# Prompt attention: the causal mask added in PSUM by VectorE instead of by a third product on TensorE

## The reference, cut to what matters

```python
def block(i):
    start = i * Q_BLOCK                                   # Q_BLOCK = 128
    logits = (jnp.einsum('bqhd,bkhd->bhqk', qb, k) * scale
              + (fq[..., None] - f_cum[:, :, None, :]))
    qpos = start + jnp.arange(Q_BLOCK)
    logits = jnp.where(qpos[:, None] >= key_pos[None, :], logits, -jnp.inf)
    probs = jax.nn.softmax(logits, axis=-1).astype(v.dtype)
    return jnp.einsum('bhqk,bkhd->bqhd', probs, v)
```

## Time and profile before

| | before |
|---|---|
| median of 3 runs | 3169.92 us (3169.56 to 3171.61) |
| the profiled execution, own time | 3169.61 us |
| its span in the trace | 3168.0 us |
| TensorE busy in the span | 3096.5 us, 98% |
| VectorE, ScalarE, GpSimd busy | 1558.5, 910.9, 261.2 us |

### The profile page before, as it was taken

The page is one execution under the profiler, slowest core; times in us unless marked ns, Lnnn a source line. Parts: engine busy times, 40 slices in busy tenths (PEclk is TensorE's granted clock), DMA queues, the critical chain, the costliest instruction groups (busy, mean ns, idle before and its releaser), DMA issues.

```text
span 3168.0 us, 52161 instructions
## 1 busy us (share of the span) xinstructions
PE 3096.5 (98%) x20550; PEld 2968.3 (94%) x20550; DVE 1558.5 (49%) x2693; ACT 910.9 (29%) x1670; POOL 261.2 (8%) x317
## 2 busy tenths in 40 slices
PE   8999999999999999999999998999999999999999
PEld 8999999999999999999987776559999999999998
DVE  4444284444444447543335555552844444544472
ACT  4111351111111116422225554343511111111262
POOL 1000010000000001000015542210100000000011
PEclk9999999999999999999999999999999999999999
DMA  2111111111111111113227774971111111111112
GB/s 99 47 47 41 47 37 45 47 47 41 47 47 41 47 61 39 42 47 118 70 46 162 131 135 172 386 300 51 41 47 41 47 47 41 47 47 40 61 48 70
DMA packets 234057, 238.93 MB, mean 75 GB/s; under 512 B 18806, under 2 KB 191862, under 8 KB 233859
## 3 DMA queue, kind: packets, MB, share of 16 engines
q1 hardware_dynamic: 209842, 156.26, 16.9%
q0 software_dynamic: 24016, 79.77, 8.5%
HBM read 201.11 MB, written 18.10 MB: 69 GB/s over the span
## 4 chain that ended last, share of the span: by engine, by line
PE 80%; DVE 4%; issue 2%; ACT 2%; DMA 1%; POOL 0%; DVEq 0%; SPq 0%; ACTq 0%; POOLq 0%
PE psum L2082 21%; PE psum L2084 21%; PE psum L2083 21%; PE psum L2638 3%; PE psum L2108 2%; PE psum L2102 2%; PE psum L2103 2%; PE psum L2622 2%; PE psum L2607 1%; PE psum L2608 1%; PE psum L2688 1%; PE psum L2740 1%; DVE xs_lo L1563 1%; PE psum L2717 0%; PE psum L2649 0%
## 5 line engine op out<-in xcount | busy, mean ns | idle before, releaser
L2082 PE MATMUL psum<-xs_hi,w_hi 128*128 128x384 f32 (+1 forms) x2784 | 911.6, 327 | 2.7 <-DVE w_lo L1339 2.4
L2084 PE MATMUL psum<-xs_hi,w_lo 128*128 128x384 f32 (+1 forms) x2784 | 908.0, 326 | 0.0
L2083 PE MATMUL psum<-xs_lo,w_hi 128*128 128x384 f32 (+1 forms) x2784 | 907.3, 326 | 0.0
L2082 PEld LDWEIGHTS psum<-xs_hi,w_hi 128*128 128x128 f32 x2784 | 522.7, 188 | 3.9 <-DVE w_lo L1339 3.7
L2083 PEld LDWEIGHTS psum<-xs_lo,w_hi 128*128 128x128 f32 x2784 | 522.7, 188 | 0.0
L2084 PEld LDWEIGHTS psum<-xs_hi,w_lo 128*128 128x128 f32 x2784 | 522.5, 188 | 0.0
L782 ACT ACTIVATE w_hi<-raw 128x1024 fp32r<-128x1024 f32 x192 | 202.4, 1054 | 622.3 <-DVEq L1355 598.4
L2084 PE MATMUL psum<-hid_hi,w_lo 128*128 128x384 f32 (+1 forms) x1056 | 346.0, 328 | 0.0
L2082 PE MATMUL psum<-hid_hi,w_hi 128*128 128x384 f32 (+1 forms) x1056 | 345.6, 327 | 0.0
L2083 PE MATMUL psum<-hid_lo,w_hi 128*128 128x384 f32 (+1 forms) x1056 | 345.1, 327 | 0.0
L1696 DVE TENSOR_TENSOR y<-y,psum 128x384 f32<-128x384 f32 x528 | 268.6, 530 | 155.3 <-PE psum L2084 155.3
(11 more groups left out here) (311 smaller groups left out, 4104.9 us busy)
## 6 DMA issues: line engine op xcount, KB each, us to landing
kpage<-in_cache_k SPq DMA_DIRECT2D x64, 512.0 KB, 8.5
v_page<-in_cache_v POOLq DMA_DIRECT2D x64, 512.0 KB, 5.7
raw<-in_w_gate SPq DMA_DIRECT2D x44, 512.0 KB, 3.7
raw<-in_w_up SPq DMA_DIRECT2D x44, 512.0 KB, 3.7
raw<-in_w_down SPq DMA_DIRECT2D x44, 512.0 KB, 3.8
raw<-in_w_in SPq DMA_DIRECT2D x24, 512.0 KB, 3.6
raw<-in_w_ple_gate SPq DMA_DIRECT2D x16, 512.0 KB, 3.8
k_hh<-kT_scratch POOLq DMA_DIRECT2D x32, 256.0 KB, 6.5
```

The costliest lines, as they stand in the source:

```text
L2082: M(out, wh, xh, start=first, stop=False)
L2083: M(out, wh, xl, start=False, stop=False)
L2084: return M(out, wl, xh, start=False, stop=last)
```

## The change

The third product is gone; the second product of the last part ends the sum and raises `s_ready`. VectorE adds the mask `causal` to the last 128 columns in PSUM, in place, raises `s_masked`, waits for it and takes the maximum. Ahead of the stage VectorE waits for `consts` to reach 6. The copies `causal_r` and `ident_r` and TensorE's wait for them go.

```diff
--- before.py
+++ after.py
@@ -168,8 +168,6 @@
     convT = misc("convT", [P, C, 2 + 2 * NB])
 
     causal = sb("causal", [P, P], F32, off)
-    causal_r = sb("causal_r", [P, P], F32R, off + 512)
-    ident_r = sb("ident_r", [P, P], F32R, off + 1024)
     wf_raw = misc("wf_raw", [P, C, H])
     wf_hi = misc("wf_hi", [P, C, H], F32R)
     wf_lo = misc("wf_lo", [P, C, H], F32R)
@@ -302,7 +300,7 @@
         fs_stored = sem("fs_stored")
         v_stored = sem("v_stored")
 
-        aug_one, mask_ready = sem("aug_one"), sem("mask_ready")
+        aug_one, s_masked = sem("aug_one"), sem("s_masked")
         head_landed = [sem(f"head_landed{i}") for i in range(2)]
         head_raw_landed = sem("head_raw_landed")
         aug_landed = [sem(f"aug_landed{i}") for i in range(2)]
@@ -1207,9 +1205,6 @@
             for hh in range(2):
                 A(k_low[hh][DH:DH + 4, :], k_raw[DH:DH + 4, :], ACT.Copy).then_inc(aug_one, 1)
                 A(q_high[hh][DH:DH + 4, :], k_raw[DH:DH + 4, :], ACT.Copy, scale=-1.0).then_inc(aug_one, 1)
-            act_e.wait_ge(consts, 6)
-            A(causal_r[:, :], causal[:, :], ACT.Copy).then_inc(mask_ready, 1)
-            A(ident_r[:, :], ident[:, :], ACT.Copy).then_inc(mask_ready, 1)
             for tb in range(NTB):
                 if tb == 8:
                     act_e.wait_ge(fs_stored, 32)
@@ -1919,8 +1914,13 @@
                 row(TR_V, tb)
 
 
+            dve.wait_ge(consts, 6)
+
             def maxes(i):
                 dve.wait_ge(s_ready, i + 1)
+                diag = slice(QBS[i % NI] * P, (QBS[i % NI] + 1) * P)
+                V.tensor_tensor(s_view(i)[:, diag], s_view(i)[:, diag], causal[:, :], ALU.add).then_inc(s_masked, 1)
+                dve.wait_ge(s_masked, i + 1)
                 V.reduce_max(nmx[:, i % 4:i % 4 + 1], s_view(i), AX_X, negate=True).then_inc(s_max, 1)
 
             def take_probT(i):
@@ -2585,7 +2585,6 @@
             pe.wait_ge(tr_dve, TR_V + NTB)
 
 
-            pe.wait_ge(mask_ready, 2)
             pe.wait_ge(f_step, 8)
 
             def scores(i):
@@ -2602,13 +2601,10 @@
                 for part in range((qb + 4) // 4):
                     k0 = 512 * part
                     k1 = min(k0 + 512, (qb + 1) * P)
-                    diag = k1 == (qb + 1) * P
                     out = psum[:, b + part, 0:k1 - k0]
                     M(out, q_hl[hh][:, qs], k_hh[hh][:, k0:k1], start=True, stop=False)
-                    M(out, q_high[hh][:, qs], k_low[hh][:, k0:k1], start=False, stop=not diag)
-                    if diag:
-                        M(psum[:, b + part, k1 - k0 - P:k1 - k0], ident_r[:, :], causal_r[:, :], start=False,
-                          stop=True).then_inc(s_ready, 1)
+                    ins = M(out, q_high[hh][:, qs], k_low[hh][:, k0:k1], start=False, stop=True)
+                ins.then_inc(s_ready, 1)
 
             def transpose_probs(i):
                 pe.wait_ge(exp_done, i + 1)
```

## The result

The changed kernel takes 3177.31 us (median of 12 runs, 3174.24 to 3180.47) where the kernel before takes 3169.22 (12 runs, 3166.98 to 3171.61). The ratio is 1.0027, 95% interval 1.0019 to 1.0034: 8.6 us slower by the ratio, 6.0 to 10.8 by its interval; the medians are 8.1 us apart. Forecast were +8.0 us and 3177.9.

What follows compares the result with a forecast made beforehand. PE bounds the stage, with holes from a PE-VectorE-PE ring three times per head: 3 x 0.33 - 0.37 = +0.62 us. Over heads 0.2 + 8.7 - 0.7 = 8.2, block by block 8.05, taken as 8.0: 3177.9 us, range 3172.5 to 3181.5.

Steps and rivals of the forecast that it cites:

- The ring: Prompt attention: PE waits three times per head for VectorE copies queued behind maxima that waited for PE; only work there counts.
- D: Time of one VectorE mask addition plus its semaphore wait, in front of each maximum: 0.33 us, between 0.20 and 0.39.
- 0.37 of 0.63 us: PE's saving per head from eight removed products: 0.63 us in all, of which 0.37 lies on the ring.
- A: PE's wait for a VectorE copy behind block 6's maximum: 0.79 us idle before, 1.05 forecast; the whole D counts.
- B: PE's wait for a copy behind block 0's maximum and two multiplications: 0.22 us before, 0.43 forecast; the whole D counts.
- +0.62: Added time per head in us: three additions of 0.33 on the ring less 0.37 of saved products.
- The waits for loads, worth 0.7 us: PE's short waits before some heads for their loads: a later PE no longer waits there, -0.7 us.
- C: PE's wait for a VectorE copy behind block 4's maximum: 0.25 us before, 0.46 forecast; the whole D counts.
- rival 1: Addition hides and PE's saving comes through: some 3.5 us faster, 3166.4, or 3160 if loads came sooner; chance 0.07.
- cheaper: Same ring, D of 0.20 to 0.28: +2.5 up to +6 us, 3172.4 to 3176; chance 0.27.
- rival 3: D 0.39 or more: +10.7 us, 3180.6; second part, additions reaching block 3's exponential, up to 3185; chance 0.15.
- Loads that become the bound (4): A head's loads, issued at the scores' semaphore and later with PE, become the bound; chance 0.01.

Runs made afterwards that it cites:

- 2: Kernel before with VectorE's mask addition put in as well, third product kept (mask added twice): 3181.04 us, ratio 1.0042 to the kernel before.
- 3: Kernel before with the addition replacing the third product only for query blocks 6, 0 and 4: 3177.43 us, ratio 1.0032 to the kernel before.
- 4: Kernel before with the addition replacing the third product only for query blocks 7, 1, 5, 3 and 2: 3168.72 us, ratio 0.9999.
- 5: Changed kernel with block 0's mask and maximum put behind the multiplications and the awaited copy: 3173.11 us, ratio 1.0014 to the kernel before.
- 1: Changed kernel with no mask at all, neither third product nor addition (probabilities not causal): 3168.24 us, ratio 0.9997 to the kernel before.
- 9: Kernel before with the first four key pages loaded behind the last head's load: 3165.20 us, ratio 0.9989 to the kernel before.
- 10: Changed kernel with the first four key pages loaded behind the last head's load: 3174.76 us, ratio 1.0020 to the kernel before.
- 6: Kernel before with the first four key pages loaded at head 13 instead of head 2: 3171.78 us, ratio 1.0006 to the kernel before.
- 7: Changed kernel with the first four key pages loaded at head 13 instead of head 2: 3176.66 us, ratio 1.0026 to the kernel before.
- 8: Third product for blocks 6, 0 and 4, addition for the others, block 0's maximum late, key pages at head 13: 3170.31 us, ratio 1.0004.
- 11: Third product for blocks 6, 0 and 4, addition for the others, block 0's maximum late, key pages behind last head's load: 3165.79 us, ratio 0.9987.

## Why the prediction was right

**The bound.** The ring PE, VectorE, PE, three times a head, is shown by 2 to 5: additions in place of products cost 0.70 us a head at blocks 6, 0 and 4 and nothing at the other five, and turning one place of the queue round takes 0.26 us a head away.

**The price of the addition.** D was put at 0.29 + 0.04; it is 0.294 + 0.034. Neither of its bounds, 0.20 and 0.39, was reached. The Trainium skill (Perfetto Trace Analysis, Optimizing Scalar/DVE Operations) has about 60 ns for a VectorE access on SBUF and about 125 ns on PSUM. Charged to the write in full, the 65 ns between them would have given 0.395. The addition, which writes PSUM, takes 8 ns more than the copy, which writes SBUF, so this case does not bear out such a charge.

**The saving.** 0.37 of 0.63 us on the ring. With the additions in place it is 0.34 (18.30 in 2 against 17.96), so the term held. With the additions absent, 1 shows 0.28, and the term that was too large there is the 0.12 of block 0, between A and B. From A to B PE takes 5.49 us in even and 5.39 in odd heads of the kernel before and 5.40 in all late heads of 1: the product's removal bought 0.09 us in every second head and nothing in the others, 0.04 on average. In odd heads the multiplications already start as soon as `rinv_row` lets them, 0.70 us behind the start of ScalarE's copy as in 5:

```profile
1899.21 0.60 ACT L1241 ACTIVATE rinv_row<-psum 128x512 f32<-128x512 f32 x1 [1.49 <-PE psum L2649]
...
1899.91 1.39 DVE L1947 TENSOR_TENSOR qo<-psum,rinv_row 64x512 f32<-64x512 f32 x2
```

So at B two paths end close together, the maximum's and ScalarE's, and the prediction saw one. Why even heads start the multiplications 0.1 us later is open.

**Per head.** Forecast +0.62; measured 17.96 against 17.32, +0.64.

**Over the stage.** The waits for loads, worth 0.7 us, were taken up as forecast: heads 3 to 14 together grow by 7.0 us where 12 x 0.64 is 7.7, and loads wait for PE now, twelve times. That the long wait before head 2 swallows part of what comes ahead of it fits 9 and 10: 9.6 us without it, 8.1 with it, though these 1.5 us are less than the medians can prove. What the sum did not hold is the spread that comes from the long wait, which makes the profiled execution 10.6 us slower than the one before while the medians are 8.1 apart. That the two numbers, 8.0 and 8.1, are so near is partly luck: the interval is 6.0 to 10.8.

**One reading was drawn up wrongly.** The waits at A, B and C were to be 1.05, 0.43 and 0.46 us; they are 1.20, 0.50 (head 12, even like the head of the 0.22) and 0.65, all longer. I had taken off only the products on the ring, as if they shortened the waits. But PE's time per head is its work and its waits: a head is 0.64 us longer with about 0.57 us less work (9.1 us in 16 heads), so the waits together must grow by 1.2. They do: by 0.41, 0.28 (0.25 in odd heads) and 0.40 at A, B and C and by 0.12 at ScalarE's copy. The sum per head does not hang on it, but the test that I wrote, that any other growth would speak against the size of the addition, was wrong: the size was right and the waits were still others. Heads 12 to 15 were forecast at 17.9 to 18.0 and are 17.96; PE's busy time was to fall by about 10 us in the stage and fell by 9.1 (9.4 between 9 and 10); VectorE's was to rise by 36 and rose by 36.3.

**The rivals.** A hidden addition (rival 1) falls with 2, a cheaper or dearer one (2 and 3) with the 294 ns; the second part of rival 3, additions that reach block 3's exponential, with the 0.98 us of 2, which leaves no room for it. Loads that become the bound (4) fall with the waits: they got more room.

## What to carry to other kernels

Before work is moved from a busy engine to a half idle one, follow the queue of the second engine: an instruction costs its full time wherever the first engine waits for something queued behind it and no other path ends at about the same time, however idle the second is on average. At the places off that ring the same instruction was free here, and where it was not, putting the awaited copy ahead of the new work gave back half of the loss here (4 of 8 us). A saving on the busiest engine is worth only what lies between its waits, here 0.28 to 0.34 of an estimated 0.63 us a head.

## What the runs showed of the hardware

- A VectorE addition that writes PSUM in place, one input in PSUM and one in SBUF, 128x128 float32: 294 ns, against 286 for a copy from PSUM to SBUF.
- Four page loads of 512 KB issued in 5.4 us held up a head's load that ran beside them, at head 2 as at head 13. PE waited 2.36 us before head 2 in the kernel before, 2.75 in the changed one and 0.73 to 4.35 in experiments 1 to 5; before head 13 it waited 2.22, 1.37 and 3.25 us in 6, 7 and 8. What sets the length is open. Loaded when no head was on its way (9 to 11), they held up none, and the part behind the stage took 1220.0 us in 9 and 1220.7 in 10, against 1219.3 and 1221.2 with the loads at head 2.
- TensorE's granted clock was 0.5 (1.2 GHz) for 3.4 or 6.8 us around the end of such a wait, and the longer stretch did not go with the longer wait: 6.8 us with 2.22, 2.75 and 4.35 us of waiting, 3.4 with 2.36, 2.54 and 3.25. With the waits of 0.73, 0.80, 1.12 and 1.37 us before head 2 or 13, and with the waits of up to 1.2 us at A, it stayed at 1.0. What decides between 3.4 and 6.8 us is open.
